# The roots of RMS and layer norms on ScalarE as exp(-0.5 ln x) instead of on VectorE

## What is computed

```python
def _rms(x, g):                     # a root over the last axis
    return x * rsqrt(mean(x * x) + 1e-6) * g
def _layernorm(x, g, b):            # x less its mean, then the root
    return xc * rsqrt(mean(xc * xc) + 1e-5) * g + b
# layer A: h = rms(x); GLU -> causal conv over 31 tokens -> layer norm over 768 channels -> silu;
#          beside it attention of rms-normed queries over a memory of 256 tokens; x += [conv; mem] @ w_out
# layer B: k, v = projections of rms(x) by norm_kv, keys rms-normed per 64 channels; h = rms(x);
#          6 heads of differential attention with rms-normed queries, their outputs rms-normed per 128;
#          beside it attention over the memory again; x += [attn; mem] @ w_out
# both:    h = rms(x); x += (gelu(conv3(h Wg)) * (h Wv)) @ w_down        (d_ff = 2816)
# memory keys, both layers: rms of the memory, projection, rms per 64 channels
```

## Time and profile before

| | |
|---|---|
| runs of the kernel, us | 1595.33 median, 1595.21 to 1600.1 |
| the profiled execution: span, mean granted clock of PE | 1595.4 us, 0.954 |
| PE busy (matmul), PEld (weight load) | 1467.6 us (92%), 1393.1 us (87%) |
| DVE busy | 959.0 us (60%) |
| ACT busy | 577.3 us (36%) |
| POOL (GpSimd) busy | 119.7 us (8%) |
| table loads on ACT | 54, of them 19 ahead of the square root (L1018) |

### The profile page before, as it was taken

One profiled execution on the slowest core, in us unless ns is written; L12 is line 12 of the kernel. 1 busy time (PEld: TensorE's weight loads), 2 busy tenths in 40 slices (PEclk: granted clock), 3 DMA queues, 4 the chain that ended last, 5 costly groups with the idle time before them and its releaser, 6 DMA issues.

```text
span 1595.4 us, 27270 instructions
## 1 busy us (share of the span) xinstructions
PE 1467.6 (92%) x10820; PEld 1393.1 (87%) x10820; DVE 959.0 (60%) x1827; ACT 577.3 (36%) x949; POOL 119.7 (8%) x133
## 2 busy tenths in 40 slices
PE   4899867899999999999999996888999999999997
PEld 3799765789999999999888884765999999999997
DVE  4789888556663664466767775217366635653662
ACT  3444434444431222223445554125243322221232
POOL 2000103210000000001100003211010000000001
PEclk8899997789999999999999998998899999999999
DMA  7121222122233233222322224431123233233222
GB/s 208 42 65 54 93 79 81 30 66 82 85 87 93 85 87 93 81 85 74 91 73 60 68 65 167 165 104 53 40 80 93 80 92 93 80 93 88 85 74 67
DMA packets 208538, 134.87 MB, mean 85 GB/s; under 512 B 4971, under 2 KB 201152, under 8 KB 208391
## 3 DMA queue, kind: packets, MB, share of 16 engines
q1 hardware_dynamic: 201319, 105.30, 23.0%
q0 software_dynamic: 7120, 28.18, 5.4%
HBM read 126.24 MB, written 7.85 MB: 84 GB/s over the span
## 4 chain that ended last, share of the span: by engine, by line
PE 72%; DVE 17%; ACT 5%; issue 3%; DMA 1%; SPq 1%; POOL 0%; POOLq 0%; ACTq 0%; DVEq 0%
PE acc L485 55%; PE acc L662 6%; DVE conv_out L1478 3%; ACT w_hi L999 2%; PE acc L963 2%; DVE w_lo L1385 2%; PE psX L751 1%; PE psX L946 1%; DVE softmax_stats L1864 1%; ACT exps L1288 1%; DVE turned L1402 1%; DVE root_row L1411 1%; PE psT L696 1%; SPq L398 1%; PE psX L844 1%
## 5 line engine op out<-in xcount | busy, mean ns | idle before, releaser
L485 PE MATMUL acc<-xa_hi,w_hi 128*128 128x272 f32 x1824 | 384.8, 292 | 10.6 <-DVE xa_lo L1416 10.1
L485 PE MATMUL acc<-xa_hi,w_lo 128*128 128x272 f32 x1824 | 378.7, 289 | 0.0
L485 PE MATMUL acc<-xa_lo,w_hi 128*128 128x272 f32 x1824 | 377.6, 289 | 0.0
L999 ACT ACTIVATE w_hi<-w_raw 128x1024 fp32r<-128x1024 f32 x194 | 205.4, 1059 | 383.1 <-PE acc L485 306.5
L485 PEld LDWEIGHTS acc<-xa_hi,w_hi 128*128 128x128 f32 x1824 | 289.1, 189 | 13.1 <-issue 10.2
L1385 DVE TENSOR_TENSOR w_lo<-w_raw,w_hi 128x1024 fp32r<-128x1024 f32 x194 | 237.6, 1225 | 84.8 <-ACT w_hi L999 83.2
L485 PEld LDWEIGHTS acc<-xa_lo,w_hi 128*128 128x128 f32 x1824 | 288.3, 190 | 0.0
L485 PEld LDWEIGHTS acc<-xa_hi,w_lo 128*128 128x128 f32 x1824 | 286.2, 190 | 0.0
L485 PE MATMUL acc<-xb_hi,w_hi 128*128 128x272 f32 x832 | 174.8, 291 | 2.0 <-DVE xb_lo L1812 2.0
L485 PE MATMUL acc<-xb_hi,w_lo 128*128 128x272 f32 x832 | 172.1, 288 | 0.0
L485 PE MATMUL acc<-xb_lo,w_hi 128*128 128x272 f32 x832 | 171.6, 288 | 0.0
(11 more groups left out here) (298 smaller groups left out, 1989.3 us busy)
## 6 DMA issues: line engine op xcount, KB each, us to landing
w_raw<-in_w_up SPq DMA_DIRECT2D x88, 512.0 KB, 3.9
w_raw<-in_w_down SPq DMA_DIRECT2D x32, 512.0 KB, 3.9
w_raw<-in_w_in_a SPq DMA_DIRECT2D x14, 512.0 KB, 4.3
w_raw<-in_w_down SPq DMA_DIRECT2D x16, 384.0 KB, 3.3
w_raw<-in_w_kv SPq DMA_DIRECT2D x12, 512.0 KB, 3.8
k_pages<-in_cache_k POOLq DMA_DIRECT2D x16, 384.0 KB, 4.3
v_pages<-in_cache_v POOLq DMA_DIRECT2D x16, 384.0 KB, 3.9
w_raw<-in_w_mem_kv SPq DMA_DIRECT2D x8, 512.0 KB, 3.9
```

The source lines that it names most:

```text
L485: last = nc.tensor.matmul(acc[slot][:, c, 0:n], w, x[:, k, c * n:(c + 1) * n], start=(k == 0 and q == 0), stop=(k == kb - 1 and q == 2))
L999: nc.scalar.activation(whi[:, slot % 2, :], wraw[:, slot, :], ACT.Copy).then_inc(w_hi_ready, 1)
```

## The change

On ACT, `root` is now two passes over all columns: `Ln` reads the sum straight from PSUM, with the mean's factor as its scale and epsilon as its bias (a column of the constants, which grow by three columns), and `Exp` with scale -0.5 then runs in place, so that every partition and column holds 1/sqrt. DVE waits for `root_ready` and uses the result. The Ln pass signals what the transpose did, that the sum was read (`sum_read`, or `acc_free` for a tile). All of DVE's `root` goes. A set of tables that is named for holding both functions is loaded ahead of time at `n0`, behind the last sigmoid (s = 11), at the memory's norm, at the start of both output sections and at the start of the last down group of the first feed-forward block.

The tiles' roots alternate between two buffers (`t1` and `rr`), and ACT waits for the multiply of two tiles before (`qk_done`). For a tile, `conv(3)` now stands ahead of DVE's wait for the root, where it stood between the narrow shift and the reciprocal. The lambda sums of DVE's setup move ahead of the wait for the first norm. Per-head variances are divided by HEAD_VAR = 8 inside the logarithm, and the seven gain columns of head norms are scaled by 8^-0.5 once, in DVE's setup. The heads' norm takes `Ln` and `Exp` over its 102 narrow columns on ACT, without the reciprocal; its transposes stay. PE's waits on `turned` become waits on `sum_read`. No transfer is moved.

```diff
 EPS, LN_EPS = 1e-6, 1e-5
+HEAD_VAR = 8.0
 LAM_INIT = 0.8 - 0.6 * math.exp(-0.3)
...
 C_ID, C_BLK, C_MASK, C_NEW, C_FOLD = 0, P, 2 * P, 3 * P, 4 * P
-C_ALL = C_FOLD + 48
+C_EPS = C_FOLD + 48
+C_ALL = C_EPS + 3
...
         RT = dict(n0=0, mem=1, ln=2, n1=3, n2=4, n3=5)
+        ROOTS = "natural_log_exp_and_others"
...
             return (psT, psX)[j % 2][:, :, 0:NPR // 2]
...
+        def root_number(what):
...
+            if what in tiles:
+                n, nq = (2, tiles[what][2])
+                return n + nq + (1 if what >= S_B else 0) + (2 if what >= S_B else 0)
+            return {"n0": 0, "mem": 1, "ln": 8, "n1": 9, "n2": 10, "n3": 25}[what]
...
+        def root_row(s):
+            return (t1, rr)[tiles[s][2] % 2]
...
                 last.then_inc(setup_filled, 1)
-            pe.wait_ge(turned, RT["n0"] + 1)
+            pe.wait_ge(sum_read, RT["n0"] + 1)
             for c in range(KD):
...
-            nrt = [0]
...
-            def root(n):
...
-                k = nrt[0]
-                nrt[0] += 1
-                w = n // 32
-                act.wait_ge(var_ready, k + 1)
-                nc.scalar.activation(small[:, 1, 0:w], small[:, 0, 0:w], ACT.Sqrt).then_inc(sd_ready, 1)
+            def root(src, n, scale, eps, out, read):
...
+                nc.scalar.activation(flat2(out[:, 0:n], n), src, ACT.Ln, bias=cst[:, C_EPS + eps:C_EPS + eps + 1],
+                                     scale=scale).then_inc(read[0], 1)
+                act.wait_ge(*read)
+                nc.scalar.activation(out[:, 0:n], out[:, 0:n], ACT.Exp, scale=-0.5).then_inc(root_ready, 1)
...
+            def model_root(norm):
+                act.wait_ge(sq_used, SQ[norm] + KD)
+                root(psX[:, :, 0:HT], T, 1.0 / D, 0, rstd, (sum_read, RT[norm] + 1))
...
                     scaled_hi(xa_hi, cc, xT[:, cc, :], pcol("norm_mix", cc), xg_hi)
-            root(T)
+            act.preload_act_table_set(ROOTS)
+            model_root("n0")
             act.wait_ge(lam_sum, 1)
...
                 if kind != "v":
-                    root(cols_of(s))
+                    n = cols_of(s)
+                    act.wait_ge(sq_used, sq_index(s) + 1)
+                    if nq >= 2:
+                        act.wait_ge(qk_done, nq - 1)
+                    root(psum2(acc[s % 2], n), n, 1.0 / (MHD * HEAD_VAR), 2, root_row(s), (acc_free, s + 1))
                     return
...
                     nc.scalar.activation(stile[:, :], gtile[:, :], ACT.Sigmoid).then_inc(sig_ready, 1)
+                if s == 2 * CC - 1:
+                    act.preload_act_table_set(ROOTS)
                 if s in tiles:
...
                         square(memT[:, c, :], MEM)
-                    root(MEM)
+                    act.preload_act_table_set(ROOTS)
+                    act.wait_ge(sq_used, SQ["mem"] + KD)
+                    root(psX[:, 0, 0:MEM], MEM, 1.0 / D, 0, rstdM, (sum_read, RT["mem"] + 1))
                     for l in range(2):
...
             mix_hi(0, mT)
-            root(T)
+            act.wait_ge(sq_used, SQ["ln"] + CC)
+            act.wait_ge(qk_done, 6)
+            root(acc[0][:, :, 0:HT], T, 1.0 / CA, 1, rr, (sum_read, RT["ln"] + 1))
             for j in range(CC):
...
             def out_section(l, gain):
+                act.preload_act_table_set(ROOTS)
                 for m in range(KD):
...
                     scaled_hi(xa_hi, m, xT[:, m, :], pcol(gain, 8 * l + m), xg_hi)
-                root(T)
+                model_root("n3" if l else "n1")
...
                         continue
+                    if l == 0:
+                        act.preload_act_table_set(ROOTS)
                     for m in range(KD):
...
                     else:
-                        root(T)
+                        model_root("n2")
...
             output_square(H)
-            root(H * T)
+            act.wait_ge(heads_var, H + 1)
+            nc.scalar.activation(small[:, 1, :], small[:, 0, :], ACT.Ln).then_inc(heads_root, 1)
+            act.wait_ge(heads_root, 1)
+            nc.scalar.activation(small[:, 2, :], small[:, 1, :], ACT.Exp, scale=-0.5).then_inc(heads_root, 1)
             mem_attention(1)
...
                                         ALU.subtract).then_inc(w_lo_ready, 1)
...
-            nrt, nturn = [0], [0]
...
-            def root(src, n, scale, eps_, out, read=None, beside=None):
...
-                k = nrt[0]
-                nrt[0] += 1
-                w = n // 32
-                if read is None:
-                    nturn[0] += 1
-                    read = (turned, nturn[0])
-                nc.vector.transpose(t1[:, 0:n], src).then_inc(read[0], 1)
-                dve.wait_ge(*read)
-                nc.vector.tensor_scalar(small[:, 0, 0:w], t1[:, 0:n].rearrange("p (a b) -> p a b", b=32)[:, :, 0],
-                                        scale, eps_, ALU.mult, ALU.add).then_inc(var_ready, 1)
-                if beside:
-                    beside()
-                dve.wait_ge(sd_ready, k + 1)
-                link(nc.vector.reciprocal(small[:, 2, 0:w], small[:, 1, 0:w]))
-                settle()
-                link(nc.vector.transpose(out, small[:, 2, 0:w].unsqueeze(2).broadcast_to((P, w, 32))))
-                settle()
...
             dve.wait_ge(setup_drained, KD + 2)
+            heads = pT[:, col["k_norm"]:NROW]
+            link(nc.vector.tensor_scalar(heads, heads, HEAD_VAR ** -0.5, None, ALU.mult))
             split_lo(0)
...
             split_lo(1)
-            dve.wait_ge(sq_used, 8)
-            root(psX[:, :, 0:HT], T, 1.0 / D, EPS, rstd[:, :])
...
             dve.wait_ge(ld_lam, 16)
...
             nc.vector.tensor_reduce(lamt[:, 1:2], lamin[:, 2, :], AX.X, ALU.add).then_inc(lam_sum, 1)
...
+            dve.wait_ge(root_ready, root_number("n0") + 1)
...
                 n = cols_of(s)
-                dve.wait_ge(sq_used, sq_index(s) + 1)
...
-                root(psum2(acc[s % 2], n), n, 1.0 / MHD, EPS, rr[:, 0:n], read=(acc_free, s + 1),
-                     beside=(lambda: conv(3)) if s < S_OUT[0] else None)
+                if s < S_OUT[0]:
+                    conv(3)
+                dve.wait_ge(root_ready, root_number(s) + 1)
                 if s < S_MEM:
...
                     out, gain = mq2[:, s - S_B - 18, :], pcol("mem_q", 1)
-                nc.vector.scalar_tensor_tensor(out=out, in0=qf[:, t % 2, 0:n], scalar=gain, in1=rr[:, 0:n],
+                nc.vector.scalar_tensor_tensor(out=out, in0=qf[:, t % 2, 0:n], scalar=gain, in1=root_row(s)[:, 0:n],
                                                op0=ALU.mult, op1=ALU.mult).then_inc(qk_done, 1)
...
                 conv_sample(0)
-                dve.wait_ge(sq_used, SQ["mem"] + KD)
-                root(psX[:, 0, 0:MEM], MEM, 1.0 / D, EPS, rstdM[:, :])
                 for l in range(2):
...
                         scaled_lo(mg_lo[l], mg_hi[l], c, memT[:, c, :], pcol("norm_mem", 8 * l + c), mg_h, mg_l, 8 * l + c + 1)
+            dve.wait_ge(root_ready, root_number("mem") + 1)
             for s in range(S_MEM, S_OUT[0]):
...
-            dve.wait_ge(sq_used, SQ["ln"] + CC)
             dve.wait_ge(ln_c, CC)
-            root(acc[0][:, :, 0:HT], T, 1.0 / CA, LN_EPS, rr[:, :])
+            dve.wait_ge(root_ready, root_number("ln") + 1)
             for j in range(CC):
...
                     scaled_lo(xa_lo, xa_hi, m, xT[:, m, :], pcol("norm_ffn", 8 * l + m), xg_hi, xg_lo, 8 * nth + m + 1)
-                dve.wait_ge(sq_used, SQ[n] + KD)
-                root(psX[:, :, 0:HT], T, 1.0 / D, EPS, rstd[:, :])
+                dve.wait_ge(root_ready, root_number(n) + 1)
...
                     if l == 0:
-                        dve.wait_ge(sq_used, SQ["n2"] + KD)
-                        root(psX[:, :, 0:HT], T, 1.0 / D, EPS, rstd[:, :])
+                        dve.wait_ge(root_ready, root_number("n2") + 1)
...
                 n = NPR if i < H else H * NSA
-                settle()
+                if i:
+                    dve.wait_ge(heads_var, i)
+                else:
+                    settle()
                 dve.wait_ge(sb_sum, i + 1)
...
                 ins = nc.vector.tensor_scalar(dst, t1[:, 0:n].rearrange("p (a b) -> p a b", b=32)[:, :, 0],
-                                              1.0 / VD, EPS, ALU.mult, ALU.add)
-                if i < H:
-                    link(ins)
-                else:
-                    ins.then_inc(var_ready, 1)
+                                              1.0 / (VD * HEAD_VAR), EPS / HEAD_VAR, ALU.mult, ALU.add)
+                ins.then_inc(heads_var, 1)
...
             output_var(H)
-            nrt[0] += 1
-            dve.wait_ge(sd_ready, nrt[0])
-            link(nc.vector.reciprocal(small[:, 2, :], small[:, 1, :]))
-            settle()
...
+            dve.wait_ge(heads_root, 2)
             link(nc.vector.tensor_scalar(small[:, 2, :], small[:, 2, :], 1.0 - LAM_INIT, None, ALU.mult))
...
                         c[row, C_NEW + g * NSA + col] = -1e30
```

(10 more changed lines are left out.)

## The result

The changed kernel takes 1574.82 us (median of 4 runs, 1571.73 to 1576.2) against 1595.53 of the kernel before (4 runs, 1595.21 to 1600.1): a ratio of 0.986, interval [0.9843, 0.9877]. That is 20.7 us faster, where the forecast was 18.0 (1577.4, range 1572 to 1587). The profiled execution took 1576.2 us, of which 1574.5 are its span, 20.9 less than the 1595.4 of before.

A forecast was written before the change was run, and what follows sets the result against it. DVE was taken to bound 174 to 256 us, PE the feed-forward blocks and 786 to 960 us. Terms (a) to (h) sum to -17.95 us, from 1595.4 to 1577.4; own range 1574 to 1583, widened to 1572 to 1587.

The forecast's parts named there:

- (a): Memory tiles, 174 to 256 us: six roots leave DVE, the bound there; -8.7 us, bounds -4.5 and -9.4.
- (b): At s = 11: the new table load stands between the sigmoid and w_hi, for which DVE already waits; +1.3 us.
- (c): The other five preloads cost 0; the memory root delays the scaled copies queued behind it on ACT, +0.2 us.
- (d): Layer norm: the root is ready sooner, DVE's six multiplies stay the longest thing; -0.9 us.
- (e): norm_kv: the root is ready sooner, so xb_lo starts earlier and PE's stand shortens; -0.8 us.
- (f): Attention stretch, 786 to 960 us: PE gets back all fifteen stands before scores and products; -5.5 us, bounds 0 and -5.5.
- (g): Last two query tiles: narrow scaling held by one POOL clear instead of two, -1.8 us; the second tile's multiply sooner, -1.25.
- (h): Output heads: a second ACT pass over 102 columns replaces DVE's reciprocal; -0.5 us.
- rival 1: 174 to 256 us: PE and the diagonals take over as the pace, half of (a) is lost; 1581.7 us, chance 0.13.
- Rival 5: PE's clock: shorter stands in (e) and around 958 us keep it higher longer, another -3; 1574.4 us, chance 0.05.
- One sign of being wrong: At key tiles: DVE waiting longer than 1.5 us for the root would speak against the prediction.
- Rivals 3 and 4: Table loads in the roots: between Ln and Exp, 1592.5 us; or both behind the sum's wait, 1610.7; chance 0.04 each.

The follow-up runs named there:

- late_roots_stage_a: The changed kernel with two more ACT passes between Ln and Exp in the six memory tiles (174 to 256 us); 1575.48 us.
- same_again: The changed kernel once more, unchanged, to measure what repeats; 1575.81 us.
- late_load: The changed kernel with the table load of s = 11 moved from ahead of w_hi to behind the w_hi of s = 12; 1572.82 us.
- no_preloads: The changed kernel without its table preloads, each Ln and Exp taking the set it is given; 1602.28 us.
- old_roots_norms: The changed kernel with the old DVE root for the four model norms, the memory norm and the layer norm; 1579.38 us.
- old_roots_layer_b: The changed kernel with the old DVE root for the 14 tiles of layer B alone; 1586.32 us.

## Why the prediction was right

Each term as the prediction put it, and what the rows and the run that isolates it gave:

| term | forecast, us | measured, us |
|---|---|---|
| (a) memory tiles | -8.7 | -8.3 to -10.0 by execution; -9.4 to -9.7 without the step that goes with the clock |
| (b) load at s = 11 | +1.3 | +1.4 |
| (c) memory root | +0.2 | too small to see (s = 0 to 10: 110.56 for 110.72; 109.4 to 110.7 in the other changed kernels with preloads) |
| (d) layer norm | -0.9 | -0.8 |
| (e) norm_kv | -0.8 | -0.9 |
| (f) stands in layer B | -5.5 | -6.7 |
| (g) last two tiles | -3.05 | -2.7 |
| (h) heads | -0.5 | -0.5 |

- (a) was right in what it rested on, DVE as the bound: DVE's own work shrank by 8.6 us, and old roots alone brought the stage back. It was sized too small: the gain reaches or passes the bound of -9.4. What made up the last microsecond, waits or gaps between the old root's instructions, was not separated. That DVE would hardly meet PE was right by a hair: late_roots_stage_a shows that rival 1's chain is nearly as long, and in same_again, at the lower clock, DVE does wait for PE in one step.
- (b): its price was the load's 1.28 us and the 0.1 us by which `w_hi` starts ahead of the sigmoid's end when no load stands between; late_load gave 1.4 back. By the page "ScalarE: Activation LUTs", section "What ACT_TABLE_LOAD costs", of the Trainium skill it would have been 2.7. The rows disagree: in no_preloads Ln ends at 842.99, the load runs from 843.00 to 844.28 and Exp starts at 844.30.
- (f) was sized too small. The attention stretch holds 8.70 us of gain, and 1.95 of these are the first part of (g), 6.99 less 8.94 us from the product with v at 936.32 (953.26 before) to the next scores; 6.7 remain for (f). The step that was mis-sized is "all 3.8 + 1.7": the idle time that the list shows is not the whole price of a stand. The windows from the scores behind one key to those behind the next, before and after:

```profile
845.30:874.05 28.75, 27.71 (x203) 24.86 (x203) 21.80 (x50) 16.02 (x34) 0.75 (x1) 1.00 0.23 65
```

```profile
832.99:860.52 27.53, 27.53 (x204) 24.86 (x203) 18.05 (x42) 13.22 (x32) 0.75 (x1) 1.00 0.23 68
```

That is 1.22 us less, where three stands of 0.45, 0.34 and 0.26 (1.05) were listed; the rest is PE's own busy time, 27.71 for 27.53 at the same granted clock.
- (g): the first scaling was held by one clear, not by two, -1.95 for -1.8. The second clear then held the scaling at 943.57, +0.6, which had no place in the sum. The last tile's multiply comes 1.3 us sooner behind its exponentials, as forecast.
- One gain had no term: from the `w_lo` behind `norm_kv` to the first scores it is 21.21 us instead of 22.23, with PE busy throughout in both, at granted clocks of 0.92 and 0.90. Neither old_roots_norms (21.20) nor old_roots_layer_b (21.30) brings it back, so its cause stays open; late_load, at a clock of 1.00, takes 19.69 there.
- The measured terms add to 18.5 to 20.2 us, by the ends of (a), and with this stretch to 19.5 to 21.2, for 20.7 by the medians. How exact that is can't be said, as the start moves by 3 us (20.7 to 24.1, cause open) and the stretch behind the attention by 7.5 us between two executions of one kernel. Rival 5 gave the clock 3 us, to one side only. That part of the sum was not to be had from one profile.
- The range owes something to luck. Its lower end, 1574 before widening, does not follow from the bounds of (a), (f) and (g): only (a) reaches below the forecast, by 0.7, to 1576.7. The time of 1574.8 lies under that. It was taken in by the widening for the clock, and what went beyond the forecast were (a), (f) and the stretch without a term.
- One sign of being wrong came true without being one: DVE waits 2.57 us for the root at key tiles, where more than 1.5 was to speak against the theory. The root takes 1.44 us from its read to the multiply, near the 1.39 forecast. The sign measured how early DVE, freed of its roots, arrives, and not how late the root is.
- Rivals 3 and 4 were kept out by the preloads alone. Had rival 3 come, its 1592.5 would have been wrong by 10. Some 4.5 of them are the memory tiles, which keep 1.5 us of gain and not 6: it counted what loads do to DVE, and left out ACT, on which the diagonals stand behind the root. Another 2.7 stand in the steps 0 to 10 (113.45 us for 110.72), where it put nothing; the rest was not traced.

## What to carry to other kernels

An operation that moves from a busy engine to an idle one is priced by what stands behind it on the new engine: here the root's lateness, the diagonals queued behind it, and the load of its tables, of which the sets must be asked for by name. Read a gain stage by stage, from landmarks that repeat; a stage in which two engines have come nearly level charges for what is added to the one that was not the bound (some 5 of 6 us here). Cover measured in one kernel is not cover in the next: what waits there may arrive later.

## What the hardware showed that was not expected

GpSimd's clears held DVE's narrow TENSOR_SCALAR (0.17 us alone) for 1.14, 1.98 and 2.03 us, to the end of the clear, in three kernels, while TENSOR_TENSOR (0.43) and TENSOR_REDUCE (0.69) took their usual time inside one. And the same 830-odd matmuls behind the attention kept PE busy for 138.3 us in one execution and for 149.5 in another of the same kernel, at a mean granted clock of 0.94 and 0.86.
